# The one-hot of a gate's first key, built token by token with its scale in the same VectorE instruction

## The chip, the cores and the metric

One core of a Trainium2 chip runs one program. The metric is the device time of that program in microseconds (us): before the change the median of three runs is 2123.35 us (2121.81 to 2123.43). Engines are named as in the profile: PE is TensorE, with PEld its weight loads, DVE is VectorE, ACT is ScalarE, POOL is GpSimd, SP issues the large transfers.

## What is computed

A decoder layer on 256 tokens of width 2048 in float32: an input projection, a Conformer convolution and a short gated convolution, an output projection with a layer norm, and then the PEER expert network, which is where the change lies. Its core, from the reference:

```python
def peer_block(x_tok, w_q, sub_keys, peer_u, peer_v):
    ...
    s1, i1 = lax.top_k(s[:, :, 0], TOPK_HALF)
    s2, i2 = lax.top_k(s[:, :, 1], TOPK_HALF)
    cand = (s1[..., :, None] + s2[..., None, :]).reshape(t, PEER_HEADS, TOPK_HALF * TOPK_HALF)
    top_s, ci = lax.top_k(cand, TOPK)
    e1 = jnp.take_along_axis(i1, ci // TOPK_HALF, axis=-1)
    e2 = jnp.take_along_axis(i2, ci % TOPK_HALF, axis=-1)
    experts = e1 * N_KEYS + e2
    g = jax.nn.softmax(top_s, axis=-1)
    u_sel = peer_u[experts]
    act = jax.nn.gelu(jnp.einsum('td,thkd->thk', x_tok, u_sel), approximate=False)
    coef = act * g.astype(act.dtype)
    v_sel = peer_v[experts]
    return jnp.einsum('thk,thkd->td', coef, v_sel)
```

There are 128 first keys, 128 second keys and so 16384 experts; each token selects 8 heads x 16 of them, 128 in all.

## The kernel before

The kernel gathers no expert. It multiplies all experts densely (`up`: x times U, then gelu, then `down`: times V) and multiplies by a matrix of gates that is zero where a token did not select an expert. The experts go by second key: `c` counts 0 to 127, and a chunk is the 128 experts that share a second key, with the first key on the partitions. The gates are kept for two quarters of 32 second keys in `gates`.

**How gates are made.** Partitions hold the 128 selections of a token, columns the tokens. For a batch of `BATCH` = 8 tokens, TensorE multiplies for each token a one-hot of the first key (`oh1`, 128 selections x 128 keys, the stationary operand) with a one-hot of the second key of one quarter (`oh2g`, 128 x 2 x 32, the moving operand); the product is the sum over selections. The gate value rides on the one-hots: its power of two (`gate_p`) multiplies `oh1`, its fraction in two float16 parts (`gate_t`) multiplies `oh2`. A quarter takes 256/8 = 32 batches, four quarters 128 batches. On VectorE one batch is `onehot2` (L976), `onehot1` (L984, the comparison with the key numbers) and `gated` (L990 multiplies `oh1` by `gate_p`, L993 makes `oh2g`). TensorE runs `gate_batch` (L1310, eight matmuls), ScalarE copies one half of the result into `gates` (L493), VectorE adds the other (L1006, `gates_add`). Both one-hot buffers are doubled (`b` is 0 or 1). In all three layouts the token is the innermost index, so the eight matmuls of a batch read both operands at a step of 8 elements.

**What runs beside it.** Weights come in units of 128 x 1024 floats. Per unit, ScalarE rounds to `w_hi` (L387, after TensorE has used up the slot's last unit), and the rest `w_lo` is made by VectorE for even slots (L602) and by GpSimd for odd slots (L361), three units ahead of TensorE. Every product is three matmuls (L1176 to L1178 in `up`, L1346 to L1348 in `down`).

**The stages with gate batches**, and the order of VectorE's work in them, which the code writes out by hand:

- The first quarter: `up_pair`, 8 rounds (7 in a loop) of 4 batches and 4 units. Per batch VectorE runs `gates_add`, then `build` for the batch two further on, then `lo` for every second unit.
- `group(0)`: 4 steps with 2 batches each.
- The steady loop: groups 1 to 22, 4 steps each, 88 steps with one batch each. One step is `coef` (L1021), `onehot2`, L1026 (`coef_lo`, the rest of the coefficients, which waits for ScalarE's L499), `onehot1`, `lo` of slot 0, `gated`, two additions `add_v` (L1064), `lo` of slot 2, `gates_add`. TensorE in a step: `down` (24 matmuls of 512 columns), first unit of `up` (24 of 256 columns), the gate batch that was built in this same step, second unit of `up`.

After that no batches are left. Engines run in order and are held to each other by counters: TensorE's `gate_batch` waits for `oh_done` and `oh_chain`.

## Time and profile before

| | |
|---|---|
| median of 3 runs | 2123.35 us |
| the profiled execution: span | 2121.8 us |
| PE busy | 2036.9 us (96%) |
| DVE busy | 1607.9 us (76%) |
| ACT busy | 907.1 us (43%) |
| POOL busy | 879.1 us (41%) |
| stage `up_pair` | about 560 to 690 us |
| `group(0)` | about 690 to 755 us |
| steady loop | about 755 to 1840 us, 12.34 us a step |

The profiled execution has no time of its own but its span from first to last instruction, 2121.8 us; the median lies 1.55 us above that span. Busy time of PE contains the latency of each matmul, so 96% does not mean that its array always streams. "Idle before" in a row is the time in which the engine did nothing before those instructions. A start in a timeline is when the instruction begins on its engine; consecutive VectorE instructions overlap by about 0.08 us in the records, so the time from one start to the next is what an instruction costs.

### The profile page before, as it was taken

What the parts mean: (1) busy time and instruction counts of PE and PEld (TensorE: products, weight loads), DVE (VectorE), ACT (ScalarE), POOL (GpSimd) and SP (SyncE); (2) the same over time, 40 slices, a digit from 0 to 9 for tenths busy, and PEclk for the clock granted to TensorE, in tenths of its full rate; (3) what the DMA queues carried; (4) which work ended last, traced back from release to release, by engine and by line L of the source; (5) the groups of instructions that cost most, each with busy time, mean ns of one, the idle gap of its engine ahead of it and who ended that gap; (6) DMA issues with size and microseconds to landing.
All of it is one profiled execution on the core that took longest, in us unless ns stands there. A gap on an engine that the chain in (4) does not pass through costs nothing.

```text
span 2121.8 us, 39656 instructions
## 1 busy us (share of the span) xinstructions
PE 2036.9 (96%) x13418; PEld 1862.0 (88%) x13418; DVE 1607.9 (76%) x2338; ACT 907.1 (43%) x1135; POOL 879.1 (41%) x358
## 2 busy tenths in 40 slices
PE   8999988898898999999999999999999999999997
PEld 8999966898898899999999999999999999989885
DVE  7999976799999876676676667667667666655787
ACT  5433343333343344444444444444444444444443
POOL 4544435355443333334334343333433434444444
PEclk9999999899999999999999999999999999999998
DMA  7554446334333455555555545555554554555554
GB/s 260 199 179 166 171 151 218 114 134 159 119 119 121 137 186 172 169 169 168 177 162 174 171 165 175 170 169 168 169 177 163 174 172 164 178 182 189 185 189 157
DMA packets 97531, 357.51 MB, mean 168 GB/s; under 512 B 10816, under 2 KB 10944, under 8 KB 96448
## 3 DMA queue, kind: packets, MB, share of 16 engines
q1 hardware_dynamic: 96896, 355.77, 50.1%
q10 hardware_dynamic: 576, 0.96, 0.1%
q8 instruction: 36, 0.59, 0.1%
q14 instruction: 23, 0.19, 0.0%
HBM read 354.59 MB, written 2.10 MB: 168 GB/s over the span
## 4 chain that ended last, share of the span: by engine, by line
PE 75%; DVE 12%; issue 9%; DMA 1%; DVEq 1%; ACT 1%; SPq 0%; ACTq 0%
PE bank L1176 11%; PE bank L1177 11%; PE bank L1178 11%; PE bank L1346 11%; PE bank L1347 11%; PE bank L1348 11%; PE bank L1310 6%; DVE cacc L639 2%; DVE w_lo L602 2%; DMA raw<-in_w_in_dram 1%; PE bank L1220 1%; PE bank L1221 1%; PE bank L1222 1%; DVE cand L882 1%; DVE acc L679 1%
## 5 line engine op out<-in xcount | busy, mean ns | idle before, releaser
L361 POOL TENSOR_TENSOR w_lo<-raw,w_hi 128x1024 fp32r<-128x1024 f32 x340 | 864.3, 2543 | 1223.4 <-ACT w_hi L387 1223.4
L387 ACT ACTIVATE w_hi<-raw 128x1024 fp32r<-128x1024 f32 x656 | 694.6, 1061 | 1014.5 <-PE bank L1178 545.7
L1176 PE MATMUL bank<-xt_hi,w_hi 128*128 128x256 f32 x2944 | 855.5, 291 | 43.2 <-DVE w_lo L602 30.0
L1177 PE MATMUL bank<-xt_lo,w_hi 128*128 128x256 f32 x2944 | 840.2, 285 | 0.0
L1178 PE MATMUL bank<-xt_hi,w_lo 128*128 128x256 f32 x2944 | 838.3, 285 | 0.0
L1176 PEld LDWEIGHTS bank<-xt_hi,w_hi 128*128 128x128 f32 x2944 | 572.6, 195 | 54.5 <-issue 26.4
L1177 PEld LDWEIGHTS bank<-xt_lo,w_hi 128*128 128x128 f32 x2944 | 571.8, 194 | 4.5
L602 DVE TENSOR_TENSOR w_lo<-raw,w_hi 128x1024 fp32r<-128x1024 f32 x315 | 393.2, 1248 | 239.3 <-ACT w_hi L387 238.3
L1178 PEld LDWEIGHTS bank<-xt_hi,w_lo 128*128 128x128 f32 x2944 | 571.3, 194 | 0.0
L1026 DVE TENSOR_TENSOR c_lo<-stash,c_hi 128x256 fp32r<-128x256 f32 x128 | 264.6, 2069 | 204.6 <-ACT c_hi L499 204.3
L1346 PE MATMUL bank<-w_hi,c_hi 128*128 128x512 f32 x1024 | 405.4, 396 | 0.0
L1347 PE MATMUL bank<-w_lo,c_hi 128*128 128x512 f32 x1024 | 404.7, 395 | 0.0
L1348 PE MATMUL bank<-w_hi,c_lo 128*128 128x512 f32 x1024 | 404.0, 394 | 0.0
L1348 PEld LDWEIGHTS bank<-w_hi,c_lo 128*128 128x128 f32 x1024 | 192.4, 188 | 46.8
L1346 PEld LDWEIGHTS bank<-w_hi,c_hi 128*128 128x128 f32 x1024 | 192.7, 188 | 41.6
L1347 PEld LDWEIGHTS bank<-w_lo,c_hi 128*128 128x128 f32 x1024 | 192.3, 188 | 41.0
L1064 DVE TENSOR_TENSOR acc<-bank,acc 128x512 f32<-128x512 f32 x254 | 162.5, 679 | 13.4 <-PE bank L1348 13.4
L639 DVE SCALAR_TENSOR_TENSOR cacc<-apad,prm,cacc x232 | 162.3, 751 | 0.2 <-DVE cacc L639 0.2
L1310 PE MATMUL bank<-oh2g,oh 128*128 128x64 f16 x1024 | 149.3, 304 | 8.8 <-issue 7.3
L1310 PEld LDWEIGHTS bank<-oh2g,oh 128*128 128x128 bf16 x1024 | 115.8, 148 | 16.5 <-issue 9.0
L1006 DVE SCALAR_TENSOR_TENSOR gates<-bank,gates 128x256 f32 (+1 forms) x128 | 90.9, 711 | 5.5 <-ACT gates L493 5.4
L990 DVE TENSOR_TENSOR oh<-oh,gate_p 128x1024 bf16<-128x1024 bf16 x128 | 89.5, 699 | 3.9
(137 smaller groups left out, 1074.5 us busy)
## 6 DMA issues: line engine op xcount, KB each, us to landing
raw<-in_u_w_dram SPq DMA_DIRECT2D x256, 512.0 KB, 3.7
raw<-in_v_w_dram SPq DMA_DIRECT2D x256, 512.0 KB, 3.3
raw<-in_w_in_dram SPq DMA_DIRECT2D x80, 512.0 KB, 4.2
raw<-in_w_out_dram SPq DMA_DIRECT2D x32, 512.0 KB, 3.7
raw<-in_w_q_dram SPq DMA_DIRECT2D x32, 512.0 KB, 3.7
xt_raw<-in_x_t_dram SPq DMA_DIRECT2D x4, 512.0 KB, 7.3
acc<-in_x_nat_dram SPq DMA_DIRECT2D x1, 2048.0 KB, 9.7
out_dram<-acc SPq DMA_DIRECT2D x5, 256.0 KB, 2.1
```

What stands on the lines that cost most here:

```text
L361: nc.gpsimd.tensor_tensor(w_lo[s][:, :], raw[:, s, :], w_hi[s][:, :].bitcast(f32), ALU.subtract).then_inc(lo_done[s], SPLIT)
L387: nc.scalar.activation(w_hi[slot_u % SPLIT][:, :], raw[:, slot_u % RAW, :], ACT.Copy).then_inc(hi_done, 1)
L602: tt(w_lo[slot_u % SPLIT][:, :], raw[:, slot_u % RAW, :], w_hi[slot_u % SPLIT][:, :].bitcast(f32), ALU.subtract).then_inc(lo_done[slot_u % ...
L639: i = stt(s, a, w, s, ALU.mult, ALU.add)
L1026: tt(c_lo[r][:, j, :], stashed(c), c_hi[r][:, j, :].bitcast(f32), ALU.subtract).then_inc(clo_done, 1)
L1176: mm(dst, hi_w[:, sl], xt_hi[:, kk, :], start=st, stop=False)
L1177: mm(dst, hi_w[:, sl], xt_lo[:, kk, :], start=False, stop=False)
L1178: i = mm(dst, lo_w[:, sl], xt_hi[:, kk, :], start=False, stop=en)
L1310: i = mm(bank[2 + b][:, 2 * t * QUARTER:2 * (t + 1) * QUARTER], oh1[b][:, :, t], oh2g[b][:, :, :, t].rearrange("p w e -> p (w e)"), start= ...
L1346: mm(dst, a1, w1, start=h == 0 and e == 0, stop=False)
L1347: mm(dst, a1, w2, start=False, stop=False)
L1348: i = mm(dst, a2, w1, start=False, stop=h == 1 and e == 1)
```

## The change

The one-hot of the first key is laid out with the key innermost (`oh1[b]` is 128 x 8 tokens x 128 keys), and made by eight `tensor_scalar` instructions, one per token: the key numbers `iota_b` (bf16) are compared with the token's key and the result is multiplied by the token's power of two, both scalars read per partition from `tab1` and `gate_p`. [...] The second VectorE pass over `oh1` (L990) and its counter `oh1_first` are gone, `oh_done` counts 8 per batch, and the matmul reads `oh1[b][:, t, :]`, 128 contiguous elements. `iota_b` is made by one more conversion ahead of the routing loop. `oh2` and `oh2g` stay as they are.

```diff
-        tab1 = sb("tab1", [P, T], f16)
+        tab1 = sb("tab1", [P, T], f32)
-        gate_p = sb("gate_p", [P, T], bf16)
+        gate_p = sb("gate_p", [P, T], f32)
-        oh1 = [sb(f"oh1_{i}", [P, P, BATCH], bf16) for i in range(2)]
+        oh1 = [sb(f"oh1_{i}", [P, BATCH, P], bf16) for i in range(2)]
...
+            nc.vector.tensor_copy(iota_b[:, :], iota[:, :]).then_inc(iota_done, 1)
...
             def onehot1(m, t0, b):
                 if not (isinstance(m, int) and m < 2):
                     dve.wait_ge(g_done, m - 1)
-                tt(oh1[b][:, :, :], iota_t[:, :, :],
-                   tab1[:, ds(t0, BATCH)].unsqueeze(1).to_broadcast([P, P, BATCH]), ALU.is_equal).then_inc(oh1_first, 1)
+                for t in range(BATCH):
+                    ts(oh1[b][:, t, :], iota_b[:, :], tab1[:, ds(t0 + t, 1)], gate_p[:, ds(t0 + t, 1)],
+                       ALU.is_equal, ALU.mult).then_inc(oh_done, 1)
             def gated(m, t0, b):
-                dve.wait_ge(oh1_first, m + 1)
-                tt(oh1[b][:, :, :], oh1[b][:, :, :],
-                   gate_p[:, ds(t0, BATCH)].unsqueeze(1).to_broadcast([P, P, BATCH]), ALU.mult).then_inc(oh_done, 1)
                 dve.wait_ge(oh_first, m + 1)
...
-                pe.wait_ge(oh_done, m + 1)
+                pe.wait_ge(oh_done, BATCH * (m + 1))
...
-                    i = mm(bank[2 + b][:, 2 * t * QUARTER:2 * (t + 1) * QUARTER], oh1[b][:, :, t],
+                    i = mm(bank[2 + b][:, 2 * t * QUARTER:2 * (t + 1) * QUARTER], oh1[b][:, t, :],
                            oh2g[b][:, :, :, t].rearrange("p w e -> p (w e)"), start=True, stop=True)
```

VectorE, the two batches that are built ahead of the `up_pair` loop, before (`L602` is a `w_lo`):

```order
L976 TENSOR_TENSOR oh2<-iota_t,tab2 128x256
L984 TENSOR_TENSOR oh1_0<-iota_t,tab1 128x1024
L990 TENSOR_TENSOR oh1_0<-oh1_0,gate_p 128x1024
L993 TENSOR_TENSOR oh2g_0<-oh2,gate_t 128x512
L602 TENSOR_TENSOR w_lo2<-raw,w_hi2 128x1024
```

and after:

```order
L977 TENSOR_TENSOR oh2<-iota_t,tab2 128x256
L986 TENSOR_SCALAR oh1_0<-iota_b,tab1,gate_p 128x128 x8
L992 TENSOR_TENSOR oh2g_0<-oh2,gate_t 128x512
L602 TENSOR_TENSOR w_lo2<-raw,w_hi2 128x1024
L977 TENSOR_TENSOR oh2<-iota_t,tab2 128x256
```

Two instructions over 1024 elements have become eight over 128; the rest of a batch stands as it stood, one line number lower.

VectorE in a step of the steady loop, from the rest of the coefficients to the additions, before (`ISA` and `REGISTER_ALU` are address arithmetic of its sequencer):

```order
L1026 TENSOR_TENSOR c_lo0<-stash,c_hi0 128x256
L984 REGISTER_ALU
L984 TENSOR_TENSOR oh1_1<-iota_t,tab1 128x1024
L601 REGISTER_ALU
L602 TENSOR_TENSOR w_lo0<-raw,w_hi0 128x1024
L989 REGISTER_ALU
L990 REGISTER_ALU
L990 TENSOR_TENSOR oh1_1<-oh1_1,gate_p 128x1024
L993 REGISTER_ALU
L993 TENSOR_TENSOR oh2g_1<-oh2,gate_t 128x512
L1064 TENSOR_TENSOR acc<-bank6,acc 128x512
L1064 TENSOR_TENSOR acc<-bank7,acc 128x512
```

and after, from the last of the eight instructions, each of which has its own `ISA` in front:

```order
L986 ISA
L986 TENSOR_SCALAR oh1_1<-iota_b,tab1,gate_p 128x128
L601 REGISTER_ALU
L602 TENSOR_TENSOR w_lo0<-raw,w_hi0 128x1024
L991 REGISTER_ALU
L992 REGISTER_ALU
L992 TENSOR_TENSOR oh2g_1<-oh2,gate_t 128x512
L1063 TENSOR_TENSOR acc<-bank6,acc 128x512
L1063 TENSOR_TENSOR acc<-bank7,acc 128x512
```

All of the work on `oh1` now stands ahead of `lo`; behind `lo` only `oh2g` is left.

## Rows read from the trace of the kernel before

**Rows 1.** The page's first line.
```profile
span 2121.8 us, 39656 instructions
```
**Rows 2.** Busy time by stage: us, then per engine, clock, share of DMA, GB/s.
```profile
560.00:690.00 130.00, 122.72 (x984) 120.27 (x983) 126.09 (x174) 54.79 (x78) 46.93 (x16) 0.97 0.37 123
755.00:1840.00 1085.00, 1085.00 (x7039) 985.96 (x7038) 746.36 (x967) 481.76 (x616) 423.38 (x176) 1.00 0.52 170
```
**Rows 3.** Groups of 755 to 1840 us: busy us, mean ns | idle before.
```profile
L1178 PE MATMUL bank<-xt_hi,w_lo 128*128 128x256 f32 x1408 | 396.9, 282 | 0.0
...
L1346 PE MATMUL bank<-w_hi,c_hi 128*128 128x512 f32 x703 | 278.4, 396 | 0.0
...
L1310 PE MATMUL bank<-oh2g,oh 128*128 128x64 f16 x704 | 102.8, 304 | 0.0
L1310 PEld LDWEIGHTS bank<-oh2g,oh 128*128 128x128 bf16 x704 | 79.6, 148 | 3.8
...
L984 DVE TENSOR_TENSOR oh<-iota_t,tab 128x1024 bf16<-128x1024 f16 x88 | 59.8, 679 | 0.0
```
**Rows 4.** Timeline of DVE, one steady step: start us, duration us, instruction.
```profile
1208.66 2.22 DVE L1026 TENSOR_TENSOR c_lo<-stash,c_hi 128x256 fp32r<-128x256 f32 x1 [1.94 <-ACT c_hi L499]
1210.80 0.68 DVE L984 TENSOR_TENSOR oh<-iota_t,tab 128x1024 bf16<-128x1024 f16 x1
1211.41 1.21 DVE L602 TENSOR_TENSOR w_lo<-raw,w_hi 128x1024 fp32r<-128x1024 f32 x1
1212.54 0.68 DVE L990 TENSOR_TENSOR oh<-oh,gate_p 128x1024 bf16<-128x1024 bf16 x1
1213.14 0.41 DVE L993 TENSOR_TENSOR oh2g<-oh,gate_t 128x512 f16<-128x512 f16 x1
1213.48 1.27 DVE L1064 TENSOR_TENSOR acc<-bank,acc 128x512 f32<-128x512 f32 x2
```
**Rows 5.** Timeline of POOL, the same step.
```profile
1213.79 2.41 POOL L361 TENSOR_TENSOR w_lo<-raw,w_hi 128x1024 fp32r<-128x1024 f32 x1 [3.19 <-ACT w_hi L387]
```
**Rows 6.** Timeline of PE, the same step.
```profile
1215.13 0.28 PE L1178 MATMUL bank<-xt_hi,w_lo 128*128 128x256 f32 x1
1215.25 1.17 PE L1310 MATMUL bank<-oh2g,oh 128*128 128x64 f16 x8
1216.17 0.37 PE L1176 MATMUL bank<-xt_hi,w_hi 128*128 128x256 f32 x1
```
**Rows 7.** Timeline of DVE, an instruction with two scalars read per partition, and the next.
```profile
267.56 0.40 DVE L726 TENSOR_SCALAR sct<-scpad,prm 128x256 f32<-128x256 f32 x1
267.88 0.48 DVE L639 SCALAR_TENSOR_TENSOR cacc<-apad,prm,cacc  x1
```
**Rows 8.** Timeline of DVE, the same kind of instruction with constants.
```profile
555.47 0.29 DVE L958 TENSOR_SCALAR gate_e<-gate 128x256 uint32<-128x256 uint32 x1
```
**Rows 9.** Line 726: duration in ns, least, median, most.
```profile
L726 DVE TENSOR_SCALAR sct<-scpad,prm x8: 401/404/2486, 135.6 to 267.6; 128x256 f32<-128x256 f32 x8
```
**Rows 10.** Timeline of DVE, one pair of batches in `up_pair`.
```profile
624.92 2.62 DVE L993 TENSOR_TENSOR oh2g<-oh,gate_t 128x512 f16<-128x512 f16 x1
...
628.60 0.70 DVE L1006 SCALAR_TENSOR_TENSOR gates<-bank,gates 128x256 f32 x1
...
629.42 0.68 DVE L984 TENSOR_TENSOR oh<-iota_t,tab 128x1024 bf16<-128x1024 f16 x1
...
630.83 0.42 DVE L993 TENSOR_TENSOR oh2g<-oh,gate_t 128x512 f16<-128x512 f16 x1
631.16 0.72 DVE L1006 SCALAR_TENSOR_TENSOR gates<-bank,gates 128x256 f32 x1
...
633.40 2.62 DVE L993 TENSOR_TENSOR oh2g<-oh,gate_t 128x512 f16<-128x512 f16 x1
```
**Rows 11.** Timeline of POOL, the same pair.
```profile
624.43 2.82 POOL L361 TENSOR_TENSOR w_lo<-raw,w_hi 128x1024 fp32r<-128x1024 f32 x1 [5.32 <-ACT w_hi L387]
```
**Rows 12.** Timeline of PE, the same pair.
```profile
627.64 1.14 PE L1310 MATMUL bank<-oh2g,oh 128*128 128x64 f16 x8 [0.57 <-issue]
```
**Rows 13.** Timeline of DVE at 738 us.
```profile
738.05 2.51 DVE L976 TENSOR_TENSOR oh<-iota_t,tab 128x256 f16<-128x256 f16 x1
```
**Rows 14.** Timeline of POOL at 738 us.
```profile
738.01 2.40 POOL L361 TENSOR_TENSOR w_lo<-raw,w_hi 128x1024 fp32r<-128x1024 f32 x1 [3.11 <-ACT w_hi L387]
```

More of the change, by code:

```diff
@@ L97, in build @@
         iota = sb("iota", [P, P], f32)
-        iota_t = sb("iota_t", [P, P, BATCH], f16)
+        iota_t = sb("iota_t", [P, QUARTER * 4, BATCH], f16)
+        iota_b = sb("iota_b", [P, P], bf16)
         ident = sb("ident", [P, P], f32)
@@ L230, in build @@
         oh_chain = sem("oh_chain")
-        oh1_first = sem("oh1_first")
         oh_done = sem("oh_done")
@@ L917, in _ @@
             dve.wait_ge(rt, R[0])
-            dve.wait_ge(iota_done, 3)
+            dve.wait_ge(iota_done, 4)
             decodes = [(half, b) for half in range(2) for b in range(TB)]
```

## The prediction

> **What bounds the kernel now.** The views were read in this order: the page, the table of stages, the groups of the steady loop, then the timelines of DVE, POOL and PE side by side for one step of that loop and for one pair of batches in `up_pair`. The page gives the span, 2121.8 us [rows 1]. In the table of stages, PE is busy through all of the 1085 us of the steady loop and DVE for 746 of them; in `up_pair` DVE is busy for 126 of 130 us and PE for 123 [rows 2]. So there are two regimes: 88 steps in which TensorE sets the pace and never waits for a gate batch (idle 0.0 before 704 gate matmuls, [rows 3]), and some 130 us in which VectorE has hardly a gap, with GpSimd's share in it: L993 takes 2.62 us instead of 0.42 whenever a GpSimd `w_lo` runs [rows 10, 11], and the gate batch then starts 0.10 us after L993's end, behind 0.57 us of idle PE [rows 12]. A VectorE instruction on two SBUF tensors that starts while a GpSimd `w_lo` is under way does not get going until that has ended; starting 0.04 us behind it is enough (2.51 us for 256 elements, [rows 13, 14]). L726, which has one tensor and two scalars, shows the same, at most 2486 ns against 401 [rows 9], so the new instructions can be held as well.
>
> **What is removed: two passes.** From the start of L984 to that of L993 it is 630.83 - 629.42 = 1.41 us where the two follow each other [rows 10]. In the steady step they stand on either side of L602: 0.61 us for L984, 0.60 for L990 [rows 4].
>
> **What is added: eight instructions with two scalars.** No row shows one on 128 two-byte elements, so its cost is put together. (a) A fixed part and a rate: L984 (1024 elements) takes 0.61 us from start to start, L993 (512) takes 13.48 - 13.14 = 0.34, so 0.53 ns an element and 0.07 us fixed [rows 4]. (b) L602, the same shape in four-byte elements, takes 1.13 us, 1.04 ns an element: two-byte elements halve the rate. (c) L958 has one tensor of four bytes and lasts 0.29 us; less the 0.08 of overlap and 0.07 fixed that is 0.14 for 256 elements, 0.55 ns each: having one tensor only also halves it [rows 8]. (d) L726 differs from L958 by its two scalars and takes 267.88 - 267.56 = 0.32 us instead of 0.21 [rows 7, 8]: 0.055 us per scalar. If (b) and (c) apply together, 128 elements stream in 0.034 us and one instruction costs 0.07 + 0.11 + 0.034, with the rounding of (d) 0.222 us; eight cost **1.78 us**. With one of the two halvings it is 0.067 us of streaming and 0.253, eight 2.02 us; with none 0.133 and 0.32, eight 2.56 us. The low end is no cost for the scalars beyond the first instruction, 8 x 0.104 = 0.83 us. I take 1.78, since each halving has its own row and the operands here meet the conditions of both. The Trainium skill, "VectorE: DVE Perf Modes", § The perf-mode tier table, has it the same way: a `tensor_scalar` in bf16 between SBUF tensors runs at 4x and `tensor_tensor` at 2x; no row here shows a 4x instruction. So VectorE gets **0.37 us more** work per batch (1.78 - 1.41), not less: the fixed part and the scalars are paid eight times.
>
> **Steady loop: the cover.** L1026 is held until POOL's first `w_lo` of the step ends; the eight instructions start where L984 did, 1210.80. L602 follows 1.78 later, at 1212.58, the `oh2g` product another 1.13 later, at 1213.71 instead of 1213.14. It ends at 1214.12, and TensorE wants it at 1215.25 [rows 6]: 1.1 us of slack are left of 1.7. Queued behind it are the additions L1064, whose banks TensorE needs two steps later, and L602's `w_lo` for the next step's first unit, which is wanted at 1219.1. Nothing is late. The one thing near is POOL's second `w_lo` at 1213.79 [rows 5]: it misses L993 by 0.65 us now and by 0.08 us after; POOL will wait for `oh2g` instead, which costs nothing. Steady loop: **0**.
>
> **`up_pair`: no cover.** One pair of batches takes 633.40 - 624.92 = 8.48 us when VectorE sets the pace [rows 10]. It holds two batches of 631.16 - 628.60 = 2.56, an L602 of 1.13, and 2.2 us in which L993 is held. TensorE needs less: two units of 24 matmuls at 0.12 us [rows 6] and two gate batches that cost 1.0 each beyond them, about 7.8 us. After, two batches are 2 x 2.93 = 5.86, with L602 6.99; held time is 2.3 (POOL's 2.41 hits one of the eight instead of L993), so 9.3 us a pair. The stage has 16 pairs. Roughly half of them run at TensorE's pace now, since a lead of two batches is eaten slowly; the lead (1.5 us) will be gone after one pair. 14 pairs x 9.3 less the lead, 128.7, against 114 us for the same stretch now: **+14**. Ends: -5 (held time falls under 0.8 and TensorE sets the pace throughout) and +22 (2.4 us held in every pair and no lead).
>
> **The rest.** `group(0)` has two batches a step and VectorE near its limit: 4 x 0.74 = **+3** (0 to 5). The conversion into `iota_b` stands in VectorE's queue ahead of the routing loop, one instruction of 0.14 to 0.29 us: **+0.3**. The sequencer has one address instruction more per token; it runs while the engine is busy with the instruction before. POOL's and SP's queues are unchanged.
>
> **The weights of the gate matmuls.** Contiguous reading could shorten a batch. The eight matmuls follow each other at 0.12 us (0.92 us for eight, [rows 6]) though each streams only 64 columns. The durations say which operand is slow: 512 columns take 396 ns, 256 take 282, so a column costs 0.45 ns and the rest 168 ns; 64 gate columns take 304 ns, so 136 ns of streaming, 2.1 ns a column [rows 3]. That is the moving operand, at its step of 8, and it stays as it is. A weight load starts with the matmul ahead and lasts 148 ns, of which little can be on the path. I take **0**; the lower end is that the load sets the pace and it falls to half, 8 x 0.06 us = 0.49 us a batch.
>
> **Sum.** 2121.8 + 0 + 14 + 3 + 0.3 = 2139.1 for the profiled execution, and with the 1.55 us by which the median lies above it 2140.7 us. A measurement of this kernel can tell about 0.2% (4 us) from no change.
>
> **Rivals.**
> *A collision in every step* (much slower). If eight instructions cost over about 1.88 us (0.235 each), `oh2g` starts 0.04 us or more behind POOL's second `w_lo` and is held until its end. As in `up_pair`, it ends 0.29 us after POOL (627.54 against 627.25, [rows 10, 11]) and the batch starts 0.10 later: 1213.79 + 2.41 + 0.39 = 1216.59 instead of 1215.25, 1.34 us of waiting TensorE. Both POOL and VectorE hang on TensorE's progress within the step, so it recurs in all 88 steps. At 2.02 us for eight, L602 would also make POOL start 0.1 late: 88 x 1.43 = 126, and `up_pair` and `group(0)` cost 10 more: 2277. At 2.56 it would be some 88 x 2.0 + 40, 2340. For it: only 0.1 us of margin, and no row with both halvings. Against: the sum above stays under, each term from a row.
> *The weight load was the bound* (faster). 88 x 0.49 = 43 us less, in the early stages nothing, since VectorE sets the pace there: 2098. For it: the load's pace equals the matmuls' pace. Against: the 304 ns. The Trainium skill, "SBUF — State Buffer", § Door 1: The DMA port swizzle, speaks of 16-byte lines, with a penalty for each access that crosses to a new one; by that rule the old layout (16 bytes a step) pays on each of the 128 weight columns and the new one on every eighth, which is this rival, while the moving operand still pays on all 64. Rows 3 agree as to the moving operand; none shows contiguous two-byte weights.
> *Scalars are free in a row* (slightly faster). At 0.83 us for eight, a batch is 0.58 shorter than now, a pair is 6.26 - 1.16 + 2.2 = 7.3 and TensorE sets the pace in `up_pair`: -5 us, `group(0)` -1: 2117. The same page on VectorE, § The TRN2 errata, counts 58 cycles and the elements over the mode for an instruction and nothing for a scalar, by which this would come out. Against: L726's 0.11 us.
> *Nothing is seen.* 2119 to 2127, if `up_pair` hides the added work.
>
> **Chances.** Forecast 0.56; collision 0.22; weight load 0.09; free scalars 0.06; nothing seen 0.07. The forecast's own range is 2128 to 2150. The range for 8 in 10 takes in the collision at its likelier size and ends at the bottom short of the weight load: 2115 to 2280. Faster by over 0.2%: 0.09 and 0.05 of the free scalars, 0.14; within: 0.07; slower: 0.79.
>
> **What would show it.** Right: eight L986 at 0.22 us from start to start; pairs of `up_pair` of about 9.3 us with PE idle before L1309; steps of 12.34 us in the steady loop, POOL's second `w_lo` lasting 2.7 instead of 2.4 because it waits for L992. Wrong: L992 of 2.6 us and idle PE before L1309 in the steady loop (collision), weight loads under 148 ns with matmuls closer than 0.12 (weights), L986 at 0.10 (scalars).

## The result

The changed kernel takes 2130.25 us (median of 13 runs, 2126.77 to 2133.99) against 2123.43 us of the kernel before (13 runs): ratio 1.0031, 95% interval 1.0023 to 1.0039. It is slower by 6.8 us, where 17.3 were forecast. The sign was right and so were most of the steps, but a gain that the sum had put at nothing took away half of the loss.

The page of the changed kernel begins:

```profile
span 2130.2 us, 41121 instructions
```

The profiled execution is 8.4 us longer than that of before, [rows 1]. The table of stages (us, then per engine busy us with the count of instructions: PE, PEld, DVE, ACT, POOL; then TensorE's granted clock as a share of 2.4 GHz, share of DMA, GB/s), answering [rows 2]:

```profile
560.00:690.00 130.00, 118.21 (x931) 114.89 (x930) 129.55 (x339) 51.66 (x73) 40.71 (x15) 0.95 0.33 113
755.00:1840.00 1085.00, 1084.10 (x7079) 984.01 (x7078) 804.60 (x1513) 482.60 (x620) 442.27 (x178) 1.00 0.52 171
```

In `up_pair` VectorE is busy for 129.6 of 130 us and TensorE's share has fallen from 122.7 to 118.2. In the steady loop VectorE has 58 us more to do (a step costs it 1.79 us for the eight in place of 0.61 + 0.60 for the two passes, [rows 4]) and TensorE is as full as it was.

Where the 8.4 us lie is read from the starts of four gate batches, the first (0), the last of `up_pair` (31), the last of `group(0)` (39) and the last of all (127). Timeline of PE, the kernel before:

```profile
559.38 1.15 PE L1310 MATMUL bank<-oh2g,oh 128*128 128x64 f16 x8 [1.50 <-DVE oh L990]
...
686.78 1.15 PE L1310 MATMUL bank<-oh2g,oh 128*128 128x64 f16 x8 [3.20 <-issue]
...
746.46 1.16 PE L1310 MATMUL bank<-oh2g,oh 128*128 128x64 f16 x8
...
1832.06 1.17 PE L1310 MATMUL bank<-oh2g,oh 128*128 128x64 f16 x8
```

and of the kernel after:

```profile
562.36 1.09 PE L1309 MATMUL bank<-oh2g,oh 128*128 128x64 f16 x8 [0.92 <-DVE oh L986]
...
701.37 1.09 PE L1309 MATMUL bank<-oh2g,oh 128*128 128x64 f16 x8 [3.87 <-DVE oh L986]
...
762.23 1.09 PE L1309 MATMUL bank<-oh2g,oh 128*128 128x64 f16 x8
...
1840.52 1.08 PE L1309 MATMUL bank<-oh2g,oh 128*128 128x64 f16 x8
```

| stretch | before, us | after, us | difference | forecast |
|---|---|---|---|---|
| start to batch 0 (routing and tables) | 559.38 | 562.36 | +3.0 | +0.3 |
| batch 0 to 31 (`up_pair`) | 127.40 | 139.01 | +11.6 | +14 |
| batch 31 to 39 (`group(0)`) | 59.68 | 60.86 | +1.2 | +3 |
| batch 39 to 127 (88 steady steps) | 1085.60 | 1078.29 | **-7.3** | 0 |
| batch 127 to the end | 289.7 | 289.7 | 0.0 | 0 |
| sum | 2121.8 | 2130.2 | +8.4 | +17.3 |

A steady step, to be laid beside [rows 4 to 6]; DVE, then POOL, then PE:

```profile
1211.15 1.87 DVE L986 TENSOR_SCALAR oh<-iota_b,tab,gate_p 128x128 bf16<-128x128 bf16 x8
1212.94 1.21 DVE L602 TENSOR_TENSOR w_lo<-raw,w_hi 128x1024 fp32r<-128x1024 f32 x1
1214.08 0.41 DVE L992 TENSOR_TENSOR oh2g<-oh,gate_t 128x512 f16<-128x512 f16 x1
...
1214.14 2.61 POOL L361 TENSOR_TENSOR w_lo<-raw,w_hi 128x1024 fp32r<-128x1024 f32 x1 [3.19 <-ACT w_hi L387]
...
1215.60 1.08 PE L1309 MATMUL bank<-oh2g,oh 128*128 128x64 f16 x8
1216.44 0.36 PE L1175 MATMUL bank<-xt_hi,w_hi 128*128 128x256 f32 x1
...
1227.85 1.09 PE L1309 MATMUL bank<-oh2g,oh 128*128 128x64 f16 x8
```

The eight instructions cost 1212.94 - 1211.15 = 1.79 us (forecast 1.78). GpSimd starts 0.06 us behind the `oh2g` product, waits for it and so lasts 2.61 us. TensorE finds its batch ready 1.1 us early. But the step is 1227.85 - 1215.60 = 12.25 us long, not 12.34, and from the batch's start to the next matmul pass 0.84 us instead of 0.92 [rows 6]. The groups of 755 to 1820 us (busy us, mean ns | idle before) show what has become quicker than in [rows 3]:

```profile
L1309 PE MATMUL bank<-oh2g,oh 128*128 128x64 f16 x704 | 95.5, 292 | 0.0
L1309 PEld LDWEIGHTS bank<-oh2g,oh 128*128 128x128 bf16 x704 | 70.3, 112 | 4.0 <-DVE oh L986 0.3
```

The weight load fell from 148 to 112 ns, the matmul from 304 to 292.

One pair of batches in `up_pair`, against [rows 10 to 12]; DVE, POOL and PE:

```profile
619.94 1.22 DVE L602 TENSOR_TENSOR w_lo<-raw,w_hi 128x1024 fp32r<-128x1024 f32 x1
...
621.89 1.87 DVE L986 TENSOR_SCALAR oh<-iota_b,tab,gate_p 128x128 bf16<-128x128 bf16 x8
...
624.80 4.09 DVE L986 TENSOR_SCALAR oh<-iota_b,tab,gate_p 128x128 bf16<-128x128 bf16 x8
628.81 0.41 DVE L992 TENSOR_TENSOR oh2g<-oh,gate_t 128x512 f16<-128x512 f16 x1
629.15 1.22 DVE L602 TENSOR_TENSOR w_lo<-raw,w_hi 128x1024 fp32r<-128x1024 f32 x1
...
625.32 2.41 POOL L361 TENSOR_TENSOR w_lo<-raw,w_hi 128x1024 fp32r<-128x1024 f32 x1 [6.13 <-ACT w_hi L387]
...
629.33 1.09 PE L1309 MATMUL bank<-oh2g,oh 128*128 128x64 f16 x8 [1.18 <-DVE oh L986]
```

The pair lasts 629.15 - 619.94 = 9.21 us. It is one of several patterns: from one L602 to the next VectorE takes between 7.0 and 11.4 us in this stage, 9.3 on average over 14 pairs. One of the second eight is caught by GpSimd's `w_lo` (the row of eight lasts 4.09 us instead of 1.87), and TensorE then stands still for 1.18 us, where it stood for 0.57.

TensorE's granted clock changes in this stage too, and the prediction did not look at it. Here is the stretch from batch 0 to batch 31 in the kernel before, in the kernel after, and in the run `contig_both`, which is described below and has the same VectorE work as the kernel after (columns as in the table of stages):

```profile
559.38:686.78 127.40, 120.12 (x969) 117.67 (x969) 123.79 (x170) 54.05 (x76) 47.55 (x16) 0.99 0.37 124
562.36:701.37 139.01, 123.28 (x969) 119.53 (x969) 138.56 (x356) 54.36 (x78) 44.51 (x16) 0.94 0.33 113
562.89:703.71 140.82, 100.64 (x969) 95.48 (x970) 140.82 (x356) 54.53 (x78) 39.99 (x16) 0.99 0.32 112
```

By the trace's record of the clock, TensorE had the lower of its two levels (1.2 GHz instead of 2.4) for 3.6 us of the stretch before and for 15.3 us after, and its idle time grew from 7.3 to 15.7 us. The lower clock is not what makes the stretch longer: in `contig_both` it is 0.99 again, TensorE is busy for only 100.6 us, and the stretch lasts 140.8 us all the same, with VectorE busy throughout.

### The profile page after: what moved, and what is told of

The parts are those of the page before. It is cut to its first block, busy times and chain, and to the rows that moved or that the text cites. A ratio compares the mean times of both kernels' runs of the same rounds, so it can differ in the third digit from the quotient of the medians.

```text
span 2130.2 us, 41121 instructions
## 1 busy us (share of the span) xinstructions
PE 2029.7 (95%) x13418; PEld 1853.2 (87%) x13418; DVE 1679.8 (79%) x3107; ACT 904.8 (42%) x1135; POOL 889.1 (42%) x358
## 4 chain that ended last, share of the span: by engine, by line
PE 73%; DVE 13%; issue 10%; DVEq 2%; ACT 1%; DMA 1%; ACTq 0%; SPq 0%
PE bank L1175 11%; PE bank L1176 11%; PE bank L1345 11%; PE bank L1346 11%; PE bank L1177 11%; PE bank L1347 11%; PE bank L1309 5%; DVE oh L986 2%; DVE cacc L639 2%; DVE w_lo L602 1%; PE bank L1219 1%; PE bank L1221 1%; PE bank L1220 1%; DVE cand L883 1%; DVE acc L679 1%
## 5 line engine op out<-in xcount | busy, mean ns | idle before, releaser
L361 POOL TENSOR_TENSOR w_lo<-raw,w_hi 128x1024 fp32r<-128x1024 f32 x340 | 874.3, 2572 | 1221.7 <-ACT w_hi L387 1221.7
L602 DVE TENSOR_TENSOR w_lo<-raw,w_hi 128x1024 fp32r<-128x1024 f32 x315 | 388.2, 1233 | 188.4 <-ACT w_hi L387 187.7
L986 DVE TENSOR_SCALAR oh<-iota_b,tab,gate_p 128x128 bf16<-128x128 bf16 x1024 | 264.8, 329 | 0.0
L639 DVE SCALAR_TENSOR_TENSOR cacc<-apad,prm,cacc x232 | 167.3, 771 | 0.2 <-DVE cacc L639 0.2
L1309 PE MATMUL bank<-oh2g,oh 128*128 128x64 f16 x1024 | 139.1, 292 | 16.6 <-DVE oh L986 15.9
L1309 PEld LDWEIGHTS bank<-oh2g,oh 128*128 128x128 bf16 x1024 | 102.8, 112 | 25.6 <-DVE oh L986 19.2
```

Of the source, the lines that this page charges most:

```text
L361: nc.gpsimd.tensor_tensor(w_lo[s][:, :], raw[:, s, :], w_hi[s][:, :].bitcast(f32), ALU.subtract).then_inc(lo_done[s], SPLIT)
L602: tt(w_lo[slot_u % SPLIT][:, :], raw[:, slot_u % RAW, :], w_hi[slot_u % SPLIT][:, :].bitcast(f32), ALU.subtract).then_inc(lo_done[slot_u % ...
L986: ts(oh1[b][:, t, :], iota_b[:, :], tab1[:, ds(t0 + t, 1)], gate_p[:, ds(t0 + t, 1)], ALU.is_equal, ALU.mult).then_inc(oh_done, 1)
L1309: i = mm(bank[2 + b][:, 2 * t * QUARTER:2 * (t + 1) * QUARTER], oh1[b][:, t, :], oh2g[b][:, :, :, t].rearrange("p w e -> p (w e)"), start= ...
```

## The experiments

Theory: VectorE's added work costs some 12 us in `up_pair` and `group(0)`, and the contiguous weights give back 0.084 us in each of the 88 steps. The rivals: the 7 us in the steady loop come from something else than the operand's layout; the loss comes from the conversion, from TensorE's lower clock (answered above) or from the code as a whole; and, kept from the prediction, the collision that was 0.1 us away.

### The layout of the weights alone

`contig_weights` is the kernel before with this edit, `strided_weights` the kernel after with the opposite one. The layout in memory is left alone in both, so the gates are not the reference's.

```diff
-                    i = mm(bank[2 + b][:, 2 * t * QUARTER:2 * (t + 1) * QUARTER], oh1[b][:, :, t],
+                    i = mm(bank[2 + b][:, 2 * t * QUARTER:2 * (t + 1) * QUARTER], oh1[b].rearrange("p a b -> p (a b)")[:, t * P:(t + 1) * P],
```

> The kernel before, with one edit: the gate matmul reads its stationary operand as 128 contiguous elements of oh1 instead of every eighth. VectorE's work is as before; the gates that come out are not the right ones, only their time is read. Theory W (the step of 8 in the weights was on TensorE's path): matmuls of a batch follow each other at 0.113 us instead of 0.122, weight loads take 0.117 instead of 0.146, a steady step takes 12.25 us instead of 12.34, and the whole is 88 x 0.084 + 8 x 0.084 = 8 us shorter, about 2115.5. Rival V (the shorter step of the changed kernel comes from something on VectorE's side): steps stay at 12.34 and the time at 2123.4.

> The changed kernel, with one edit: the gate matmul reads the new oh1 at a step of 8 again (the gates are not the right ones, only the time is read). Theory W: steps back to 12.34 us, the loss on VectorE in the early stages stays, the whole is 8 us longer than the changed kernel: about 2138. Rival V: no change, about 2130.

Measured: 2117.22 us for the kernel before with contiguous weights, ratio 0.9965 (0.9951 to 0.9979) to the 2124.32 us of before in the same group of runs; 2139.76 us for the kernel after with strided weights, ratio 1.0076 (1.0062 to 1.0090). Weight loads in the steady loop, contiguous and strided:

```profile
L1310 PEld LDWEIGHTS bank<-oh2g,oh 128*128 128x128 bf16 x704 | 70.3, 112 | 3.8
```
```profile
L1309 PEld LDWEIGHTS bank<-oh2g,oh 128*128 128x128 bf16 x704 | 79.6, 148 | 3.8
```

They are those of the kernels after and before. The steps are 12.25 and 12.34 us. So the gain in the steady loop is that of the weights' layout: the whole kernel changes by 7 us in the one pair and by 9.5 us in the other (1.0076 against 1.0031). The 88 steps account for 7.3 and 7.4 us of that, and 1.5 us of the second lie between batches 0 and 39. In that early stretch the contiguous weights give nothing to the kernel before (188.1 us against 187.1): VectorE sets the pace there.

### The conversion alone

`conversion_only` is the kernel before with `iota_b` and its conversion ahead of the routing loop, which nobody reads.

```diff
+            nc.vector.tensor_copy(iota_b[:, :], iota[:, :]).then_inc(iota_done, 1)
-            dve.wait_ge(iota_done, 3)
+            dve.wait_ge(iota_done, 4)
```

> The kernel before plus only the conversion of the key numbers to bf16 ahead of the routing loop. In the changed kernel TensorE is 3 us behind already before the first gate batch. If that comes from this instruction, which moves VectorE's routing work against GpSimd's w_lo, about 2126 and VectorE's first one-hot at 560 instead of 557 us; if it is chance of the run or of the new tables, 2123.5.

Measured: 2126.16 us, ratio 1.0002 (0.9993 to 1.0011): no change that can be told. Its first gate batch starts 1.7 us later than that of before:

```profile
561.05 1.16 PE L1312 MATMUL bank<-oh2g,oh 128*128 128x64 f16 x8 [0.44 <-DVE oh L992]
```

Of this start there are 14 profiles. With the kernel before's code up to there it lies at 559.38, 557.88, 558.66, 561.48, 555.96 and 558.0 us; with that of the kernel after at 562.36, 562.89, 559.87, 560.32, 558.17, 561.98 and 556.9. The spread within one code is 6 us, presumably since which VectorE operation of the routing stage meets a GpSimd `w_lo` differs from kernel to kernel; this was not tried. So the +3.0 of the one profile can be that alone; the means differ by 1.8 us, and whether that is an effect of the change stays open.

### The moving operand, and both

`contig_moving` is the kernel before with `oh2g` read as 64 contiguous elements, `contig_both` the kernel after with the same edit; again only the reading is changed, not the layout.

```diff
-                           oh2g[b][:, :, :, t].rearrange("p w e -> p (w e)"), start=True, stop=True)
+                           oh2g[b].rearrange("p w e t -> p (w e t)")[:, 2 * t * QUARTER:2 * (t + 1) * QUARTER], start=True, stop=True)
```

> The kernel before, in which the gate matmuls read the moving operand oh2g as 64 contiguous elements and the weights oh1 at their step of 8 (its layout in memory is left as it was, so the gates are not the reference's; all else runs as before). Measured so far: both strided 0.122 us a matmul, weights contiguous 0.113, both contiguous 0.030. Theory 1 (the moving operand sets the pace and the strided weights add 0.009 us to a matmul): 0.035 to 0.045 us a matmul, eight in 0.3 us, a step about 11.7 us, 2068 to 2080 us. Theory 2 (each operand at a step of 8 costs about as much by itself, and the two overlap, so that the slower one hides the other): the pace stays at 0.09 to 0.12 us, steps at 12.1 us or more, 2105 to 2120 us.

> The changed kernel, with the moving operand of the gate matmul also read as contiguous elements (the gates are not the right ones, only the time is read). My prediction had the moving operand as what sets the pace of a batch, at 2.1 ns a column. By that the matmuls now come at 0.06 us or less and a steady step is 0.4 us shorter: about 2130 - 96 x 0.4 = 2092. Rival: the weight load still sets the pace, 0.11 us stays, and the time stays at 2130.

Measured: 2086.19 us in one run for `contig_moving`, and 2080.23 us, ratio 0.9781 (0.9765 to 0.9797), for `contig_both`, 12 us under what was expected of it. `contig_both` carries VectorE's slower early stages (its batch 39 comes at 764.75 us). Timeline of PE and groups of PEld, first with the moving operand contiguous alone, then with both:

```profile
1209.56 0.69 PE L1310 MATMUL bank<-oh2g,oh 128*128 128x64 f16 x8
...
L1310 PE MATMUL bank<-oh2g,oh 128*128 128x64 f16 x704 | 60.7, 230 | 0.0
L1310 PEld LDWEIGHTS bank<-oh2g,oh 128*128 128x128 bf16 x704 | 51.2, 165 | 3.8
```
```profile
1207.72 0.41 PE L1309 MATMUL bank<-oh2g,oh 128*128 128x64 f16 x8
...
L1309 PE MATMUL bank<-oh2g,oh 128*128 128x64 f16 x720 | 36.6, 194 | 0.2 <-issue 0.2
L1309 PEld LDWEIGHTS bank<-oh2g,oh 128*128 128x128 bf16 x720 | 26.0, 98 | 4.5 <-issue 0.4 <-DVE oh L986 0.3
```

From the first to the last of the eight, over seven:

| weights / moving operand | ns from one matmul to the next | matmul, ns | weight load, ns | step, us |
|---|---|---|---|---|
| step 8 / step 8 (before) | 125 | 304 | 148 | 12.34 |
| contiguous / step 8 (after) | 113 | 292 | 112 | 12.25 |
| step 8 / contiguous | 66 | 230 | 165 | 11.93 |
| contiguous / contiguous | 31 | 194 | 98 | 11.65 |

Both theories of `contig_moving` missed (0.035 to 0.045 us, and 0.09 or more): it is 0.066. Each operand at a step of 8 costs TensorE time by itself: the moving one 82 ns over 31, the weights 35 ns, and the two together 94 rather than 117, so they overlap in part. The step of the weights costs 35 ns a matmul when the moving operand is contiguous and 12 ns when it is not. The prediction's reading that the moving operand sets the pace holds in kind, but the weights are not hidden behind it.

The Trainium skill, "SBUF — State Buffer", § Door 1: The DMA port swizzle, has lines of 16 bytes and a penalty for each access that crosses to a new one. The two operands at 16 bytes a step agree with that in kind (82 and 35 ns for 64 and 128 columns); the page gives no size, and these runs show that of the two penalties only part adds up. The 31 ns with both contiguous lie near the 25 ns that the Trainium skill, "TensorE: Matmul & The Clock Gate", § Back-to-back issue gap, gives for up to 64 columns at 2.4 GHz, a figure for the matmuls without their weight loads. The steady loop runs at that level throughout (granted clock 1.00 in its stage's row).

### What the scalars and the element's size cost

`constants` replaces the two per-partition scalars, `f32_keys` the bf16 key numbers.

```diff
-                    ts(oh1[b][:, t, :], iota_b[:, :], tab1[:, ds(t0 + t, 1)], gate_p[:, ds(t0 + t, 1)],
+                    ts(oh1[b][:, t, :], iota_b[:, :], 3.0, 2.0,
```
```diff
-                    ts(oh1[b][:, t, :], iota_b[:, :], tab1[:, ds(t0 + t, 1)], gate_p[:, ds(t0 + t, 1)],
+                    ts(oh1[b][:, t, :], iota[:, :], tab1[:, ds(t0 + t, 1)], gate_p[:, ds(t0 + t, 1)],
```

> The kernel after with the two per-partition scalars of the eight instructions replaced by the constants 3.0 and 2.0; the gates are therefore not the reference's, all else runs as it did. It measures what the scalars cost. Theory (0.055 us for each scalar of each instruction): eight cost 0.8 to 0.9 us instead of 1.79, a pair of batches in up_pair falls from 9.2 us to some 7.3 us and TensorE sets the pace there, batch 31 comes at 685 to 690 us instead of 701, and the time is 2108 to 2116 us: the steady loop keeps the 12.25 us a step of contiguous weights. Rival (the cost of 0.224 us an instruction is a fixed part of the instruction or of its address arithmetic on the sequencer, not the scalars): eight stay at 1.6 to 1.8 us and the time at 2127 to 2131 us.

> The kernel after, but the eight one-hot instructions compare with the float32 key numbers instead of their bf16 copy, so that one of the prediction's two halvings is gone. Theory (two-byte operands halve the rate, and a batch's oh2g that starts 0.04 us or more behind GpSimd's second w_lo is held until its end): eight instructions cost 2.0 to 2.05 us instead of 1.79, 0.253 each; the oh2g product starts 0.1 to 0.2 us behind GpSimd, is held to about 2.6 us in all 88 steps of the steady loop, the gate batch starts late, a step takes about 13.6 us instead of 12.25, and the time is 2230 to 2275 us. Rival 1 (the margin opens again by itself, since GpSimd waits its turn or drifts later with TensorE): steps stay at 12.25 to 12.4 us, only up_pair and group(0) get 5 to 10 us longer, 2135 to 2145 us. Rival 2 (a float32 key operand costs no rate at all): eight cost 1.79 us and the time is that of the kernel after, 2130 us.

Timeline of DVE, a steady step with constants:

```profile
1214.11 0.90 DVE L986 TENSOR_SCALAR oh<-iota_b 128x128 bf16<-128x128 bf16 x8
1214.92 1.21 DVE L602 TENSOR_TENSOR w_lo<-raw,w_hi 128x1024 fp32r<-128x1024 f32 x1
```

and one with float32 keys, with POOL's row:

```profile
1213.87 2.13 DVE L986 TENSOR_SCALAR oh<-iota,tab,gate_p 128x128 bf16<-128x128 f32 x8
1215.92 1.21 DVE L602 TENSOR_TENSOR w_lo<-raw,w_hi 128x1024 fp32r<-128x1024 f32 x1
1217.06 0.41 DVE L992 TENSOR_TENSOR oh2g<-oh,gate_t 128x512 f16<-128x512 f16 x1
...
1216.86 2.88 POOL L361 TENSOR_TENSOR w_lo<-raw,w_hi 128x1024 fp32r<-128x1024 f32 x1 [3.19 <-ACT w_hi L387]
```

With constants eight cost 0.81 us, 0.101 each (forecast of the low end 0.104), so a per-partition scalar costs (0.224 - 0.101) / 2 = 0.06 us. With float32 keys eight cost 2.05 us, 0.256 each: the 0.032 us more are those of one lost halving on 128 elements. The prediction's cost model stands in the terms that were tried, the scalars and the halving for two-byte elements. How the 0.101 us divide into a fixed part and streaming, and the halving for a single tensor, were not tried by themselves.

The times: `constants` 2100.19 us, ratio 0.9893 (0.9878 to 0.9908), 8 us under the expectation's lower end. From batch 0 to batch 31:

```profile
556.90:672.75 115.85, 115.07 (x969) 113.65 (x969) 94.97 (x356) 52.06 (x76) 36.93 (x15) 1.00 0.41 136
```

The stretch takes 116 us, not 127 as before, and TensorE is busy in all but 0.8 of them. Its own pace in `up_pair` is thus 3.74 us a batch, 7.5 us a pair; 31 x 0.084 = 2.6 us of the 11.5 are the contiguous weights', so the kernel before loses some 9 us there to VectorE, not the 5 that the prediction's third rival put on it. Most of the 9 is TensorE's idle time (7.3 us before), and the granted clock of 0.99 before against 1.00 here has a part in it. `group(0)` (batch 31 to 39) takes 55.7 us here at a clock of 1.00, against 59.7 before at 0.94, although TensorE is busy in 59.3 of these too. Some 0.7 us of the 4 are the contiguous weights'; the rest goes mostly with the lower clock, and what lowers it there was not tried. `f32_keys` takes 2142.94 us, ratio 1.0083 (1.0068 to 1.0099), with steps of 12.25 us: rival 1 of its expectation, 87 us under the theory's lower end. Its product starts **0.20 us behind** GpSimd's `w_lo`, and it is not held: it lasts 0.41 us, and GpSimd waits for 0.48 (2.88 instead of 2.40). The collision did not come, though the prediction's condition for it (0.04 us behind) was met.

### How late the product may be

`late_2` and `late_4` are the kernel after with two and four more passes of `onehot2` into spare tiles, ahead of the eight, in the steady loop only.

```diff
+                        for d in spare:
+                            tt(d[:, :, :], iota_t[:, ds(key0, QUARTER), :],
+                               tab2[:, ds(t0, BATCH)].unsqueeze(1).to_broadcast([P, QUARTER, BATCH]), ALU.is_equal)
                         onehot1(m, t0, j % 2)
```

> The kernel after with two more VectorE passes of 0.2 us (the comparison of onehot2 into spare tiles that nobody reads) ahead of the eight instructions in each step of the steady loop. The oh2g product then starts some 0.35 us behind GpSimd's second w_lo, with VectorE's own w_lo (L602) under way when GpSimd's starts. Theory A, the prediction's rule (an instruction that starts 0.04 us or more behind GpSimd is held until its end): the product lasts 2.2 us or more, TensorE waits and steps take 13.3 to 13.8 us, 2240 to 2270 us. Theory B (GpSimd, once it has started under a VectorE w_lo, waits for it, and the product directly behind goes first): the product stays at 0.41 us, GpSimd's w_lo lasts about 3.0 us, steps stay at 12.25 us, 2128 to 2134 us.

> The same with four more passes, so that the oh2g product starts about 0.75 us behind GpSimd's second w_lo, as far as the delayed instructions of up_pair did. Theory A: as in the run before it, 13.3 to 13.8 us a step, 2240 to 2275 us. Theory B: product 0.41 us, GpSimd's w_lo 3.4 us, steps 12.25 us, since TensorE wants the batch 1.1 us after the product's end in the kernel after; 2128 to 2134 us. If the two runs part, what decides is how long GpSimd has been waiting when the VectorE instruction in front ends, and the time at which they part lies between 0.35 and 0.75 us.

Timeline of DVE and POOL in a step of `late_4`:

```profile
1209.52 1.22 DVE L603 TENSOR_TENSOR w_lo<-raw,w_hi 128x1024 fp32r<-128x1024 f32 x1
1210.65 0.42 DVE L993 TENSOR_TENSOR oh2g<-oh,gate_t 128x512 f16<-128x512 f16 x1
...
1209.91 3.42 POOL L362 TENSOR_TENSOR w_lo<-raw,w_hi 128x1024 fp32r<-128x1024 f32 x1 [3.19 <-ACT w_hi L388]
```

One run each: 2132.35 and 2128.16 us, steps of 12.25 us in both. GpSimd starts 0.74 us ahead of the product, while VectorE's own `w_lo` is under way, and waits for both (3.42 us). Theory B holds as far as it was tried, 0.74 us. Theory A, the prediction's rule, holds in other places: in `up_pair` `oh2g` was held with 0.49 us behind GpSimd and L990 in front of it [rows 10, 11].

It is tempting to put this down to the instruction in front, a `w_lo` in the steady loop and L990 or one of the eight in `up_pair`. The traces speak against that. In `conversion_only` the comparison for the second key stands directly behind VectorE's `w_lo` (L603) and is held, DVE and then POOL:

```profile
560.86 1.22 DVE L603 TENSOR_TENSOR w_lo<-raw,w_hi 128x1024 fp32r<-128x1024 f32 x1
562.00 2.49 DVE L978 TENSOR_TENSOR oh<-iota_t,tab 128x256 f16<-128x256 f16 x1
...
561.91 2.43 POOL L362 TENSOR_TENSOR w_lo<-raw,w_hi 128x1024 fp32r<-128x1024 f32 x1 [13.21 <-ACT w_hi L388]
```

GpSimd was 0.09 us ahead there. In the kernel after the same comparison (L977, at 563.31 us), also behind a `w_lo`, lasts 0.29 us although GpSimd is 0.57 us ahead. So neither the instruction in front nor GpSimd's lead decides alone, and what does stays open. The Trainium skill, "SBUF — State Buffer", § Who interferes with whom, has whichever of the two engines issues first go first; GpSimd started 0.74 us ahead of L993 here and was served behind it, so, as far as starts in the trace tell the order of issue, the measurement speaks against that as the whole rule.

### The change in the steady loop only

`hybrid` is the kernel before up to the end of `group(0)`; the 88 steps of the steady loop have the eight instructions and the contiguous weights. `tab1f` and `gate_pf` are float32 copies of the two tables, made between the two parts.

```diff
-                        onehot1(m, t0, j % 2)
+                        dve.wait_ge(g_done, m - 1)
+                        tokens(m, t0, j % 2)
...
+            def tokens(i, t0, b):
+                oh = oh1[b].rearrange("p k t -> p (k t)").rearrange("p (t k) -> p t k", t=BATCH)
+                for t in range(BATCH):
+                    ts(oh[:, t, :], iota_b[:, :], tab1f[:, ds(t0 + t, 1)], gate_pf[:, ds(t0 + t, 1)],
+                       ALU.is_equal, ALU.mult).then_inc(oh_done, 1)
```

> The kernel before in up_pair and group(0) (two passes over 1024 elements, both gate operands read at a step of 8), the kernel after in the steady loop alone (eight instructions, weights contiguous). Theory (the change gains 0.084 us in each of 88 steps by the contiguous weights, loses some 12 us in up_pair and group(0) where VectorE sets the pace, and the few us of the routing stage are chance): 2114 to 2119 us, under the kernel before by 5 to 9, with steps of 12.25 us and batch 31 at 686 to 690 us. Rival (the loss is not tied to VectorE's extra work in the early stages but to the kernel as a whole, for instance the code or the address arithmetic): 2124 us or more.

Measured: 2117.16 us, ratio 0.9971 (0.9959 to 0.9984), with steps of 12.25 us and batch 31 at 686.92 us: the half of the change that gains, without the half that loses. The stretch from batch 0 to batch 39, over all profiles, says the same of the other half. With the two passes: before 187.1 us, `contig_weights` 188.1, `contig_moving` 186.4, `hybrid` 187.7, `hybrid_both` 186.2, `token_major` 188.6, `conversion_only` 189.1. With the eight instructions: after 199.9, `strided_weights` 201.3, `late_2` 201.9, `late_4` 199.8, `contig_both` 201.9. `f32_keys`, with its 0.26 us more a batch, takes 215.2 and `constants` 171.5.

### Both operands contiguous in the steady loop

`hybrid_both` adds to `hybrid` that `oh2g` lies token by token in the steady loop, VectorE going through it in the old order. `token_major` instead lets VectorE write it, and `oh2` (as `oh2t`), in the order in which they lie; the broadcast operands are then read at a step of 0.

```diff
-                    tt(oh2g[b][:, :, :, :], oh2[:, :, :].unsqueeze(1).to_broadcast([P, PARTS, QUARTER, BATCH]),
-                       gate_t[:, :, ds(t0, BATCH)].unsqueeze(2).to_broadcast([P, PARTS, QUARTER, BATCH]),
-                       ALU.mult).then_inc(oh_chain, 1)
+                    tt(oh2g[b].rearrange("p w e t -> p (w e t)").rearrange("p (t w e) -> p t w e", t=BATCH, w=PARTS),
+                       oh2t[:, :, :].unsqueeze(2).to_broadcast([P, BATCH, PARTS, QUARTER]),
+                       gate_t[:, :, ds(t0, BATCH)].rearrange("p w t -> p t w").unsqueeze(3)
+                       .to_broadcast([P, BATCH, PARTS, QUARTER]), ALU.mult).then_inc(oh_chain, 1)
```

> The kernel of the run before this one (hybrid), and in the steady loop the moving operand oh2g is also written token by token in memory, so that the eight gate matmuls read both operands contiguously there; VectorE writes oh2g at a step of 64 elements instead of 1. Theory (the moving operand at a step of 8 costs some 0.6 us a batch of TensorE, and VectorE has room in the steady loop but not in up_pair): a batch's eight matmuls follow in 0.2 us instead of 0.79, a step takes 11.6 to 11.7 us, the oh2g product costs 0.6 us instead of 0.34 or less, and the time is 2055 to 2070 us. Rival 1 (the strided write of oh2g makes it end late or lets it meet GpSimd's w_lo, as the margin was only 0.06 us): idle TensorE before L1330 in the steady loop and 2090 us or more. Rival 2 (at the shorter step another engine or the DMA sets the pace): steps of 11.9 us or more, with waits on weights or on w_lo.

> up_pair and group(0) as in the kernel before; in the steady loop oh1, oh2 and oh2g all lie token by token, so that VectorE writes and TensorE reads all of them contiguously; only the broadcast operands of VectorE (the token's second key, the gate's fraction) are read at a step of 0. It gives the reference's output. The run with the step-64 write (2.08 us for the oh2g product) showed that the layout must be contiguous for the writer too. Theory: the oh2g product costs at most 0.60 us (1.04 ns an element and 0.07 fixed), onehot2 at most 0.34, GpSimd waits its turn behind them, the eight gate matmuls take 0.2 us, steps take 11.65 us, and the time is 2058 to 2070 us, under the kernels before and after. Rival (the operand at a step of 0, or the longer product, brings back the cost of the strided write or a meeting with GpSimd): idle TensorE before L1338 or so in the steady loop, steps of 12.2 us or more, over 2110 us.

`hybrid_both`: 2157.62 us, ratio 1.0159 (1.0145 to 1.0173). Its DVE, POOL and PE in a step:

```profile
1206.67 2.49 DVE L1000 TENSOR_TENSOR oh2g<-oh,gate_t 128x512 f16<-128x512 f16 x1
1208.75 1.52 DVE L1079 TENSOR_TENSOR acc<-bank,acc 128x512 f32<-128x512 f32 x2
...
1206.73 4.15 POOL L364 TENSOR_TENSOR w_lo<-raw,w_hi 128x1024 fp32r<-128x1024 f32 x1 [3.19 <-ACT w_hi L390]
...
1209.26 0.39 PE L1330 MATMUL bank<-oh2g,oh 128*128 128x64 f16 x8 [0.91 <-issue]
```

The product costs 1208.75 - 1206.67 = 2.08 us instead of 0.34. GpSimd did not hold it (it starts behind and waits, 4.15 us): it is the write at a step of 64 two-byte elements, 4 ns an element. The eight matmuls are quick (0.20 us from first to last) but start 0.91 us late. That is rival 1 of the expectation in its effect, by a price that nobody had put on the write.

`token_major`: **2063.10 us** (5 runs), ratio 0.9716 (0.9703 to 0.9729), 60 us under the kernel before, and it computes what the reference does. DVE and PE in a step:

```profile
1209.98 0.69 DVE L1007 TENSOR_TENSOR oh2g<-oh2t,gate_t 128x512 f16<-128x512 f16 x1
1210.58 1.28 DVE L1087 TENSOR_TENSOR acc<-bank,acc 128x512 f32<-128x512 f32 x2
...
1211.51 0.41 PE L1338 MATMUL bank<-oh2g,oh 128*128 128x64 f16 x8
...
1223.16 0.41 PE L1338 MATMUL bank<-oh2g,oh 128*128 128x64 f16 x8
```

The product costs 0.60 us (a broadcast at a step of 0 as the innermost index costs VectorE the halving of two-byte elements, no more), steps take 11.65 us and TensorE does not wait.

## Why the prediction was right in kind and wrong in size

- **What bounds the kernel**: right. TensorE sets the pace in the steady loop, VectorE in `up_pair`; `hybrid` and `constants` bear both out.
- **Eight instructions cost 1.78 us**: 1.79, and by the two terms that were tried: 0.06 us a scalar and 0.03 us for a halving; the rest is 0.10 us.
- **`up_pair` +14**: +11.6. The pairs take 9.3 us on average, as worked out, though in uneven lengths. Over all profiles the stretch is 138.0 to 140.8 us with the eight and 126.4 to 129.6 with the two passes, so the difference between two profiles lies anywhere from 8 to 14. The prediction left out the granted clock, which fell from 0.99 to 0.94 here; as VectorE sets the pace, that cost nothing that can be seen.
- **`group(0)` +3**: +1.2; over both stages together the profiles with the eight instructions lie at 199.8 to 201.9 us and those with the two passes at 186.2 to 189.1, so 11 to 16 of the 17 forecast. That VectorE sets the pace in `group(0)` is not shown: TensorE is busy for 59.3 of 59.7 us there before and for 58.3 of 60.9 after, at clocks of 0.94 and 0.96.
- **Conversion +0.3**: no change that can be measured; the +3.0 at the first batch lies within the 6 us by which profiles with the same code differ there.
- **Steady loop 0: the weights.** This step failed. "A weight load starts with the matmul ahead and lasts 148 ns, of which little can be on the path. I take 0." The reading of the moving operand as the slower one was right (82 ns against 35), but that did not make the other free: 12 ns of each matmul were the weights', 0.084 us a batch over its seven intervals, 7.3 us in 88 steps. With 7.3 taken off, the forecast is 2133.4 against 2130.25 measured. The remaining 3 us are the 4.2 by which `up_pair` and `group(0)` were put too high, less the 2.7 that the start took more, and 1.5 because the changed kernel's median lies 0.05 us above its profiled span, where the sum added 1.55. The lower end of that term (0.49 us a batch) was considered, but only as a rival in which the load was the whole bound; what lay between, both operands on the path in part, was given no value. No row of before separates the two, so the term needed a middle value, not a zero.
- **The collision, 0.22**: did not come, and the eight stayed under the 1.88 us that it asked for. Its condition was also wrong: at 0.20, 0.33 and 0.74 us behind GpSimd the product went through in the steady loop. The rule was taken from other places in the kernel, and it does not hold everywhere. The upper end of the range, 2280, rested on it.
- **The weight load was the bound, 0.09**: its signs came (weight loads of 112 ns, matmuls 0.113 us apart) and the direction was right, but its price was six times too large (43 us). With the moving operand at a step of 8, the step of the weights costs 12 ns a matmul and not the 60 of this rival.
- **Scalars free in a row, 0.06**: refuted by `constants`. Its price was too small as well: -9 us in `up_pair` instead of -5, apart from the weights.

## What to carry to other kernels

Where small matmuls follow each other, work out what one costs with each of its two operands contiguous: that the slower one sets the pace doesn't make the other one free, and here the layout of the moving operand, which the change left as it was, was worth 54 us (2117.16 to 2063.10) against the weights' 7. A layout pays only if its writer too goes through it contiguously (0.60 us against 2.08). And a change that gains in one stage and loses in another belongs in the first alone: the same edit gave +6.8 us everywhere and -6.9 us in the steady loop only.

## What the runs showed of the hardware that was not expected

- A two-byte operand read by TensorE at a step of 8 elements costs it 82 ns a matmul as 64 moving columns, 35 ns as 128 columns of weights, and 94 ns together (113, 66 and 125 ns a matmul over 31).
- A VectorE product that writes two-byte elements at a step of 64 elements took 2.08 us for 512, against 0.34 with all operands packed and 0.60 with a broadcast innermost and a packed write.
- In the steady loop GpSimd waits for the VectorE product that stands directly behind a float32 `w_lo`, even where GpSimd starts 0.20, 0.33 or 0.74 us earlier (it then lasts 2.88, 3.01 and 3.42 us in place of 2.40). The product was held in none of these steps. Elsewhere the same GpSimd instruction held the next VectorE instruction for some 2.5 us: behind a bf16 pass, in the row of eight `tensor_scalar`, and in `conversion_only` behind a `w_lo` too. What decides is open.
